# A ring of four weight slots split in two: four landing slots and two working pairs, in a hybrid decoder layer on one core

## The reference, cut to what matters

```python
h = x
n = rmsnorm(h, norm_mix_w)
u = n @ w_in                                    # 2048 x (A 6144 | B 6144 | C 10304 | gates 6144)
y_a = short_conv_mixer(u_a, conv_a_w) @ w_branch_a
y_b = stick_breaking_attention(u_b) @ w_branch_b          # 16 heads of 128
y_c = mamba2_ssd(u_c, ...) @ w_branch_c                   # 64 heads in 8 groups, width 4096
h = h + (g_a * y_a + g_b * y_b + g_c * y_c) @ w_out       # g = sigmoid(u_g)
h = h + peer_ffn(rmsnorm(h, norm_ffn_w), ...)             # 16384 experts, all weights read
out = rmsnorm(h, final_norm_w)
```

## Time and profile before

| | us |
|---|---|
| three runs | 3562.46, 3566.07, 3569.57 |
| the profiled execution | 3566.07, its span 3564.3 |
| busy: PE, PEld, DVE, ACT | 3472.8 (97%), 3194.7 (90%), 2281.4 (64%), 1721.8 (48%) |
| ScalarE idle before upper parts (L121) | 751.4, of it 508.7 for transfers of `w_in` |
| VectorE idle before lower parts (L126) | 702.6, of it 702.0 for upper parts |
| TensorE waited for lower parts (L126), whole span | 23.8, 25 times, the longest 6.3 |
| stage A, branch A, B, branch B | 311.3, 181.3, 318.9, 179.8 |
| C, branch C, output projection | 540.6, 277.8, 103.4 |
| granted TensorE clock over the span | 0.997 of full |

### The profile page before, as it was taken

The page is one execution under the profiler, slowest core; times in us unless marked ns, Lnnn a source line. Parts: engine busy times, 40 slices in busy tenths (PEclk is TensorE's granted clock), DMA queues, the critical chain, the costliest instruction groups (busy, mean ns, idle before and its releaser), DMA issues.

```text
span 3564.3 us, 69907 instructions
## 1 busy us (share of the span) xinstructions
PE 3472.8 (97%) x23289; PEld 3194.7 (90%) x23289; DVE 2281.4 (64%) x2908; ACT 1721.8 (48%) x2502; POOL 27.6 (1%) x32
## 2 busy tenths in 40 slices
PE   7999999999999999999999999999999999999998
PEld 7999889998899999988879989899999988887887
DVE  4555444444557777775545999988889855554555
ACT  4444444444435445454445434447777644444444
POOL 0000000000000000000000000000000000000000
PEclk9999999999999999999999999999999999999999
DMA  6666665556665545456667567676666677667665
GB/s 174 176 176 177 189 178 156 158 156 184 192 183 158 151 147 158 151 145 193 188 196 208 153 159 171 157 183 160 158 159 159 166 193 193 192 193 213 193 193 166
DMA packets 482776, 620.18 MB, mean 174 GB/s; under 512 B 76641, under 2 KB 341185, under 8 KB 481473
## 3 DMA queue, kind: packets, MB, share of 16 engines
q1 hardware_dynamic: 482624, 618.14, 63.3%
HBM read 613.64 MB, written 4.19 MB: 173 GB/s over the span
## 4 chain that ended last, share of the span: by engine, by line
PE 84%; DVE 7%; DMA 3%; ACT 2%; SPq 2%; issue 2%; DVEq 0%; ACTq 0%
PE bank L79 27%; PE bank L80 26%; PE bank L81 26%; PE bank L1691 3%; DVE w_lo L1537 2%; DMA w_raw<-in_peer_down 2%; PE bank L2112 2%; DVE w_raw L1530 1%; DVE f_lo L126 1%; DMA f_raw<-in_w_in 1%; ACT f_hi L121 1%; SPq L449 1%; DMA f_raw<-in_w_out 0%; SPq L525 0%; ACT c_xpad L682 0%
## 5 line engine op out<-in xcount | busy, mean ns | idle before, releaser
L126 DVE TENSOR_TENSOR f_lo<-f_raw,f_hi 128x768 fp32r<-128x768 f32 (+2 forms) x640 | 746.3, 1170 | 702.6 <-ACT f_hi L121 702.0
L121 ACT ACTIVATE f_hi<-f_raw 128x768 fp32r<-128x768 f32 (+2 forms) x640 | 646.1, 1016 | 751.4 <-DMA f_raw<-in_w_in 508.7
L79 PE MATMUL bank<-xT_hi,f_hi 128*128 128x256 f32 x2560 | 739.1, 289 | 28.1 <-DVE f_lo L126 13.4
L80 PE MATMUL bank<-xT_lo,f_hi 128*128 128x256 f32 x2560 | 724.3, 283 | 0.0
L81 PE MATMUL bank<-xT_hi,f_lo 128*128 128x256 f32 x2560 | 724.2, 283 | 0.0
L79 PE MATMUL bank<-xT_hi,w_hi 128*128 128x256 f32 x2048 | 590.5, 288 | 20.9 <-DVE w_lo L1537 20.9
L80 PE MATMUL bank<-xT_lo,w_hi 128*128 128x256 f32 x2048 | 579.0, 283 | 0.0
L81 PE MATMUL bank<-xT_hi,w_lo 128*128 128x256 f32 x2048 | 578.9, 283 | 0.0
L1629 DVE TENSOR_TENSOR w_lo<-w_raw,w_hi 128x1024 fp32r<-128x1024 f32 x256 | 313.6, 1225 | 344.4 <-PE bank L81 336.3
L79 PEld LDWEIGHTS bank<-xT_hi,f_hi 128*128 128x128 f32 x2560 | 490.7, 192 | 40.5 <-DVE f_lo L126 13.4
L80 PEld LDWEIGHTS bank<-xT_lo,f_hi 128*128 128x128 f32 x2560 | 491.1, 192 | 1.9 <-issue 1.7
(11 more groups left out here) (268 smaller groups left out, 4922.4 us busy)
## 6 DMA issues: line engine op xcount, KB each, us to landing
w_raw<-in_peer_down SPq DMA_DIRECT2D x1024, 128.0 KB, 3.4
w_raw<-in_peer_up SPq DMA_DIRECT2D x1024, 128.0 KB, 2.6
f_raw<-in_w_in SPq DMA_DIRECT2D x1024, 96.0 KB, 2.4
f_raw<-in_w_in SPq DMA_DIRECT2D x256, 256.0 KB, 2.9
f_raw<-in_w_in SPq DMA_DIRECT2D x384, 128.0 KB, 2.7
f_raw<-in_w_branch_c SPq DMA_DIRECT2D x256, 128.0 KB, 2.7
f_raw<-in_w_branch_a SPq DMA_DIRECT2D x128, 128.0 KB, 2.8
f_raw<-in_w_branch_b SPq DMA_DIRECT2D x128, 128.0 KB, 2.7
```

The lines of the kernel that those rows point to most:

```text
L79: nc.tensor.matmul(out, lhs[0], rhs[0], start=start, stop=False, skip_group_check=True)
L80: nc.tensor.matmul(out, lhs[0], rhs[1], start=False, stop=False, skip_group_check=True)
L121: nc.scalar.activation(self.hi[u % 4][:, 0:cols], self.raw[u % 4][:, 0:cols], ACT.Copy).then_inc(self.hi_done, 1)
L126: nc.vector.tensor_tensor(self.lo[u % 4][:, 0:cols], self.raw[u % 4][:, 0:cols], self.hi[u % 4][:, 0:cols].bitcast(F32), ALU.subtract).the ...
```

## The change

The ring keeps its 8 slots and its addresses. Four slots remain for landing, `raw[u % 4]`. The other four become two for upper parts and two for lower parts, `hi[u % 2]` and `lo[u % 2]`, so the lower part has a place of its own. Two waits change. The load of unit n waits for `lo_done` to reach n - 3: VectorE has read the raw slot of unit n - 4. The upper part of unit n waits, beside its transfer, for `used` to reach n - 1: TensorE is done with unit n - 2. The matmuls and all hooks are the same. The five places where matmuls read the ring change from `u % 4` to `u % 2`; one of them is shown.

```diff
             def __init__(self):
                 self.raw = [place(f"f_raw{i}", [P, SLOT // 4], at_ring + i * SLOT) for i in range(4)]
-                self.lo = [place(f"f_lo{i}", [P, SLOT // 4], at_ring + i * SLOT, F32R) for i in range(4)]
-                self.hi = [place(f"f_hi{i}", [P, SLOT // 4], at_ring + (4 + i) * SLOT, F32R) for i in range(4)]
+                self.hi = [place(f"f_hi{i}", [P, SLOT // 4], at_ring + (4 + i) * SLOT, F32R) for i in range(2)]
+                self.lo = [place(f"f_lo{i}", [P, SLOT // 4], at_ring + (6 + i) * SLOT, F32R) for i in range(2)]
...
             def room(self, sp, n):
                 if not (isinstance(n, int) and n < 4):
-                    sp.wait_ge(self.used, n - 3)
+                    sp.wait_ge(self.lo_done, n - 3)
 
             def split_hi(self, act, n, quads, u, cols):
 
                 act.wait_ge(self.raw_full[u % 4], (quads + u // 4 + 1) * 64)
-                nc.scalar.activation(self.hi[u % 4][:, 0:cols], self.raw[u % 4][:, 0:cols],
+                if not (isinstance(n, int) and n < 2):
+                    act.wait_ge(self.used, n - 1)
+                nc.scalar.activation(self.hi[u % 2][:, 0:cols], self.raw[u % 4][:, 0:cols],
                                      ACT.Copy).then_inc(self.hi_done, 1)
 
             def split_lo(self, dve, n, u, cols):
                 dve.wait_ge(self.hi_done, n + 1)
-                nc.vector.tensor_tensor(self.lo[u % 4][:, 0:cols], self.raw[u % 4][:, 0:cols],
-                                        self.hi[u % 4][:, 0:cols].bitcast(F32),
+                nc.vector.tensor_tensor(self.lo[u % 2][:, 0:cols], self.raw[u % 4][:, 0:cols],
+                                        self.hi[u % 2][:, 0:cols].bitcast(F32),
                                         ALU.subtract).then_inc(self.lo_done, 1)
...
                         last = tri_matmul(bank[m // 2][:, (m % 2) * T:(m % 2 + 1) * T],
-                                          (fl.hi[u % 4][:, at], fl.lo[u % 4][:, at]), (xT_hi[:, u, :], xT_lo[:, u, :]),
+                                          (fl.hi[u % 2][:, at], fl.lo[u % 2][:, at]), (xT_hi[:, u, :], xT_lo[:, u, :]),
```

More of the change, by code:

```diff
@@ L1750, in b_unit @@
                         tri_matmul(bank[m // 2][:, (m % 2) * T:(m % 2 + 1) * T],
-                                   (fl.hi[u % 4][:, at], fl.lo[u % 4][:, at]), xs,
+                                   (fl.hi[u % 2][:, at], fl.lo[u % 2][:, at]), xs,
                                    start=u == 0 and m % 2 == 0, stop=u == KD - 1)
@@ L1758, in b_unit @@
                         last = tri_matmul(V[:, tb * T:(tb + 1) * T], (xT_hi[:, u, t], xT_lo[:, u, t]),
-                                          (fl.hi[u % 4][:, at], fl.lo[u % 4][:, at]),
+                                          (fl.hi[u % 2][:, at], fl.lo[u % 2][:, at]),
                                           start=u == 0 and tb == 0, stop=u == KD - 1)
@@ L1910, in branch_unit @@
                                    (yT_hi[:, y0 + k, t], yT_lo[:, y0 + k, t]))
-                            last = tri_matmul(bank[pair[tb]][:, :], lhs, (fl.hi[m % 4][:, at], fl.lo[m % 4][:, at]),
+                            last = tri_matmul(bank[pair[tb]][:, :], lhs, (fl.hi[m % 2][:, at], fl.lo[m % 2][:, at]),
                                               start=k == 0, stop=k == (KD if kind == "g" else kb) - 1)
```

## The result

The changed kernel takes 3590.76 us (median; 3586.07 to 3593.02), the kernel before, run beside it, 3564.27 us: a ratio of 1.0068, 95% interval 1.0053 to 1.0085. The forecast was 3590.0 us. Measured again, beside three of the experiments, the ratio was 1.0070 (1.0056 to 1.0083; run 8). The granted clock is 0.998 in the profiled execution, 0.997 in that of before.

What follows compares the result with a forecast made beforehand. TensorE, 97% busy, bounds the kernel; two slots fail to cover other ScalarE and VectorE work between splits. 3566.07 + 37.1 of costs - 13.4 gained = 3589.8 us, forecast 3590; eight-in-ten range about 3572 to 3612.

Steps and rivals of the forecast that it cites:

- B, 21.4 us: Stage B: softplus after units 6 and 7 and exponents at unit 12 outlast TensorE's pace, 3.05 us in each of 7 passes.
- A, 3.8 us for restarts and convs: Stage A: two conv visits on VectorE and restarts in every second unit cost 0.48 us per pass, 8 passes; bounds 0 to 10.
- Earlier loads, 13.4 us: Loads issued earlier gain 4.0 us in A, 3.2 in B, 0.9 in C, 3.8 in the output projection, 1.5 in restarts.
- Output projection, 3.8 of that: Earlier loads gain 2.9 us at unit 10, whose load queues behind x, and 0.9 at unit 3.
- Branches, 11.9 us: Gates cost 5.0 us, sigmoids 1.7, branch A's dt steps 1.8, branch B's softplus and exponents 0.9, branch C's first 24 units 2.5.
- so plain units of any size stay hidden: Claim that units without other work fit TensorE's pace: slack 0.07 us at 768 columns, 0.14 at 1024, 0.55 at 1280.
- The forecast tour: One round of two units through ScalarE, VectorE and matmuls at 1024 columns: 5.30 us against TensorE's 5.44.
- C, 0: Stage C: no cost, lower parts of units 6 to 15 stay 0.4 us or more ahead of TensorE; upper bound 4 us.
- The signs to look for: TensorE's lower-part waits 23.8 to about 45 us, B's 3.2 to some 22; wrong if B's doesn't rise or A's units exceed 2.2.
- The faster one: Whole kernel: the tour is faster than the hooks need and only earlier loads show, 3552.7 us; chance 0.06.
- The slower one: Whole kernel: a hop of 0.15 us makes the ring of two bind every unit, 3627 us; chance 0.10.
- The third: Attention matmuls in B give further slack, leaving 1 us per pass: 3575 us, or 3571 with A free; chance 0.12.

Runs made afterwards that it cites:

- run 8: The changed kernel itself, unaltered, measured again beside other experiments against the kernel before: ratio 1.0070 (1.0056 to 1.0083).
- run 2: Changed kernel with B's softplus split into pieces behind successive units and its weights one unit later: 1.0019 of the kernel before, 3571 us.
- run 1: Changed kernel with the loads' wait put back to the count of used units: 1.0109 of the kernel before, 3603 us.
- run 3: Changed kernel with the two waits ahead of an upper part swapped, used count first, then load: 1.0071 of the kernel before.
- run 5: Changed kernel with upper and lower parts made in two halves, VectorE starting after the first upper half: 1.0006 of the kernel before.
- run 6: Changed kernel with an extra 16-column ScalarE copy before each upper part: 1.0145 of the kernel before, 3614.35 us.
- run 4: Changed kernel with the same bytes laid out by stage, three or four upper slots in A, B and branches: 0.9971 of the kernel before, 3554 us.

## Why the prediction was right, point by point

- **B, 21.4 us (3.05 in each of 7 passes).** Right. Passes of 43.01 us for a forecast of 39.9 + 3.05, and run 2 takes 3.01 per pass away by moving nothing but that work. The three places are the ones named.
- **A, 3.8 us for restarts and convs.** Right in size: 35.93 for a plain pass against 35.56 with four slots is 0.37, 3.0 in eight. The units behind the two convs come 0.11 and 0.10 late, as forecast, the rest is a few hundredths at every second unit.
- **Earlier loads, 13.4 us.** Right in sum: run 1 loses 14 us, give or take some 8. By stage not: A gave 5.1 and not 4.0 (its first two passes, 40.78 and 37.74 before, 37.66 and 35.71 after, held more than the recorded waits), B 1.4 and not 3.2, C 0 and not 0.9, the output projection 6.9.
- **Output projection, 3.8 of that.** The term was read from one execution. The time from x's issue to unit 10's upper part was 13.05 before, and 10.92 and 13.44 in two executions of the changed kernel: the stage gained 7.5 in one and 3.5 in the other. The issue of x came 3.3 us earlier, measured from the start of unit 9's matmuls, where 2.9 was forecast; but the time behind it spreads over 3.1 us (10.3 to 13.4 in the nine profiles in which x is loaded in one piece), nearly as much as the term.
- **Branches, 11.9 us (5.0 + 1.7 + 1.8 + 0.9 + 2.5).** Mis-sized: 16.7. This is also above the range of 7 to 16 that the forecast gave them. The step that failed is "so plain units of any size stay hidden". At 1024 columns they come 2.748 us apart in branch A, 8 units in 21.98 to 22.04 us where 21.76 stood before. The forecast tour was 5.30 us; the medians of branch A give 2.91 + 0.10 + 1.09 + 1.22 + 0.16, about 5.49, or 2.745 per unit. Two terms were too small. The hop of 0.04 was read in B's loop; in the branches, which are written out without a loop, it is 0.10, and run 3 shows that it comes from the place of the added wait, which the forecast put at nothing. And from the end of a lower part to the first matmul it is 0.16 and not 0.05. The start of a unit is late before any idle time is recorded: with the lower part 0.16 us ahead plain units come 0.028 late, with 0.21 (run 3) 0.021, with 0.5 (run 5) not at all. Runs 3, 5 and 6 show the three sides of this: 3.4 us back in the branches for 0.06 off the hop, TensorE's pace of 2.72 with a tour 0.36 shorter, and 11.3 us more in the branches for 0.12 added. The dt steps came out as forecast: branch A's second eight units took 29.32 for 27.55, 1.8 us.
- **C, 0.** Right: 541.8 for 541.9 us, passes 69.03 for 69.04.
- **The signs to look for.** B's wait of 22 us is 16.3, at units 7, 8 and 13 as forecast, and the sum over the whole span 33.3 where I said 45: I added lateness, but the profile counts idle time alone, 0.16 us less for each wait and the restart besides, and nothing for the plain units of the branches. Times were right and the waits that should show them too high. The wait at unit 10, forecast as 3.4, was 0.9 in the first profile and 3.4 in the second. Neither sign of being wrong came: B's wait rose, and the plain units of A (5 to 15 of a pass) are 2.17 us apart, below the 2.2 named. C's length stayed.
- **The rivals.** The faster one (only the earlier loads show, 3552.7) fell: even with B's work spread the kernel is at 1.0019. Three or four upper slots give what it promised for two: 3554 (run 4). The advice of the Trainium skill to double-buffer (Trainium Kernel Development and Optimization, Best Practices) held here for C (541.8 us for 541.9) and for the transfers (2.9 us of ScalarE's 894.6 idle before upper parts), and not where an engine does other work between two refills (17.8 us in B). The slower one (the ring of two binds every unit, 3627) had a true core in the branches, and run 6 shows what it would have taken: 0.12 us more in the tour give 3614. The third (half of B's cost covered, 3575) fell with B's passes: they grew by 3.1 us and not by 1.

The sum was met to 0.8 us with the branches 4.8 under and the gains of A and the output projection over their forecast by 7. It was also added to an execution of 3566.07 us, 1.8 above the median that the result is set against. Part of that closeness is luck. (A smaller slip: 3.34 - 2.72 - 0.14 + 0.1 for a sigmoid is 0.58 and not 0.55; the 1.7 for three stands.)

## What to carry to other kernels

Before a ring is made shorter, compare every gap between two refills on each engine with the consumer's time per unit, not the engines' busy shares: one gap of 3.26 against 2.16 us, met seven times, cost 7 us, and the 128 units of A, whose tour only just fits, 3. The cure is cheap: cut the work in between into pieces shorter than the free time, size slots by the stage and not by the widest tile, or begin the second engine on half a tile. When a sum of waits is used to price a change, add what each late start costs besides its recorded idle time, here about 0.25 us.

## What the runs showed of the hardware that I had not expected

- Two waits ahead of one instruction are not free when the late one is not on the instruction itself: 0.10 us from the matmul's end to the activation's start instead of 0.04 (run 3; the median over a branch).
- A unit's matmuls took 2.41 us (768 columns) when the lower part ended under 0.1 us before them, 2.35 at 0.10 to 0.15 and 2.32 from 0.15 on; at 1024 columns 3.02, 2.94, then 2.91 from 0.15 to 0.25 and 2.88 beyond (medians over those units of the changed kernel that follow another unit directly). By these figures nothing is lost from about 0.15 us on at 768 columns, and from somewhere beyond 0.2 at 1024. Which of its steps needs the time wasn't tested.
- A ScalarE copy of 16 columns takes 0.21 us by itself but delays the next instruction by 0.12 only; two halves of 512 columns take 1.16 us together, one of 1024 takes 1.06.
- A load queued behind 2 MB of x came 10.3 to 13.4 us after x's issue in the nine profiles that have it. What sets it within that range stays open.
